# Second pass of a split-precision attention score on 64 rows: two matmuls, one for each bank, with keys' and queries' parts doubled

## Chip, cores and metric

One core of a Trainium2 chip runs the kernel. The metric is the device time of one execution in microseconds; the median of three runs of the kernel before is 688.32 us (688.25 to 689.17).

## What is computed

One pre-norm residual layer with stick-breaking attention, and a final RMSNorm. 1024 tokens, width 1024, 16 heads of 64, all in float32.

```python
def stick_breaking_attention(q, k, v):          # per head, for each block of 128 queries
    z = jnp.einsum('bhqd,bhkd->bhqk', qb, kf) * d ** -0.5
    log_beta = jax.nn.log_sigmoid(z)
    log_1m = jnp.where(mask, log_beta - z, 0.0)              # mask: key before query
    after = lax.cumsum(log_1m, axis=3, reverse=True) - log_1m
    a = jnp.where(mask, jnp.exp(log_beta + after), 0.0)
    return jnp.einsum('bhqk,bhkd->bhqd', a, vf)

def sb_mixer(h, w_in, w_out):
    q, k, v, gate = jnp.split(h @ w_in, 4, axis=-1)
    o = stick_breaking_attention(heads(q), heads(k), heads(v))
    return (o * jax.nn.silu(gate)) @ w_out

x = x + sb_mixer(rmsnorm(x, norm_g), w_in, w_out)
return rmsnorm(x, final_g)
```

## The kernel before

**Precision.** Every float32 operand of a product is held as a high part, rounded to float32r, and a low part, the difference. A product is the sum of float32r matmuls: high by high, high by low, low by high. For the projections these are three matmuls of 128 rows (`project`, L522). For the scores a head has only 64 rows (HD = 64), so high and low part lie one above the other on 128 partitions: `q_of(par, hh)` holds the high part of q of head hh on rows 64 hh to 64 hh + 63 and the low part on the other 64. `k_of(par, hh, False)` is laid out in the same way; `k_of(par, hh, True)` is the same with its halves exchanged. One matmul with each gives high by high plus low by low, and high by low plus low by high.

**Staging.** Heads go in pairs, p = 0 to 7 (par = p % 2 picks one of two buffers in `arena`). A pair has 16 slots: slot s has head hh = s // 8 and query block i = s % 8 of 128 queries, with 128 (i + 1) keys; these are the widths of the scores. Each slot interleaves the scores of that block, a third of a projection of the next pair (k, v, q, then gate; 12 matmuls of 512 columns), transposes of earlier attention weights (`t_ps`) and their products with v (`o_ps`). All engines walk the slots in the order that is written in the code, each with its own queue, and wait on counting semaphores. The helper `over_pairs` runs slot 0 to 15 for pair 0, for pairs 1 to 6 in a loop, for pair 7, and a tail. In pair 7 (545 to about 605 us in the profile) there is no next pair to project, and output projections fill the slots.

**Scores** (`scores`, L618): the block's queries are the stationary operand, keys stream. The result `z_ps[s % 2]` has two banks of 512 columns; `chunks` cut the width at the bank border. Block 4 (640 keys) starts at column 256, so that its parts have 256 and 384 columns; block 5 has 512 and 256, block 6 512 and 384, block 7 512 and 512. Per bank there are two matmuls, with `k_of(..., False)` and `k_of(..., True)`: four for each of blocks 4 to 7.

**After the scores** ScalarE takes two sigmoids of z (L847, L849), VectorE a running product (L1075), GpSimd the product of both (L1211), whose result PE transposes (L681); ScalarE (L832) and VectorE (L1044) take the transposes out of `t_ps` as high and low part for the product with v (L669).

**Splitting k and q.** ScalarE evacuates a projection to `stage` (L757) and writes the high part (L777; at the start VectorE does, L975); VectorE writes the low part, two heads in two instructions (`heads_lo`, L986). That counts `qk_split`: 4 a pair, k's two halves first, q's two last. SyncE then exchanges the halves of k by four DMAs of 256 KB (`swap_k`, L398), after `qk_split` for both halves of k and after the scores of the pair before last. It does so in slot 5 for the next pair, and once before slot 0 for pair 0.

**SyncE's queue** carries in this order: loads of x and of the first weights; `swap_k(0, 0)`; then per slot the weight load of slots with s % 4 < 2 (`load_w`, L388, which waits until GpSimd, L1178, has released the buffer), stores of outputs in slots 3 and 7 (L424), `swap_k` in slot 5. Loaded weights are split by ScalarE in slots with s % 4 in (1, 2) (L784) and GpSimd (L1178).

Of the kernel before, what the change touches and what calls it, by code (L numbers as in the profile page):

```python
# [18 lines left out]
F32 = mybir.dt.float32  # L19
F32R = mybir.dt.float32r  # L20
U8 = mybir.dt.uint8

P = 128
D = 1024
S = 1024
HEADS = 16
HD = D // HEADS
PAIRS = HEADS // 2
KB = D // P
HALF = 512  # L30
GQ = HALF // P
SLOTS = 16
# [45 lines left out]
def is_tail(p):  # L78
    return isinstance(p, int) and p == PAIRS


def is_first(p):
    return isinstance(p, int) and p == 0


def wait(eng, sem, value):

    if not isinstance(value, int) or value > 0:
        eng.wait_ge(sem, value)
# [94 lines left out]
def z_offset(i):  # L184

    return 2 * P if P * (i + 1) == HALF + P else 0


def stick_breaking_layer(nc, x, norm_g, w_in, w_out, final_g, out):
# [3 lines left out]
    with ExitStack() as ctx:  # L193
        def sb(name, shape, dt=F32):
            return ctx.enter_context(nc.sbuf_tensor(name, shape, dt))
# [4 lines left out]
        def sem(name):  # L200
            return ctx.enter_context(nc.semaphore(name))
# [6 lines left out]
        w_raw = sb("w_raw", [P, 2, HALF])  # L208
        a_g = [sb("a_group0", [P, GQ, HALF]), sb("a_group1", [P, GQ, S])]
        aT = sb("aT", [P, 2, 2, HALF], F32R)  # L210
        aT_pad = sb("aT_pad", [P, 2, 2 * P], F32R)
        stage = sb("stage", [P, 2, HALF])
        gate = sb("gate", [P, S])
# [21 lines left out]
        def q_of(par, hh):  # L235
            return arena[:, par, 0, hh * S:(hh + 1) * S]

        def k_of(par, hh, swapped):
            return arena[:, par, 2 if swapped else 1, hh * S:(hh + 1) * S]

        def v_of(par):
            return arena[:, par, 3, :].rearrange("p (b x d) -> p b x d", b=KB, x=4)
# [32 lines left out]
        qk_split = sem("qk_split")  # L275
        gate_sig = sem("gate_sig")
        gate_ready = sem("gate_ready")
        k_swapped = sem("k_swapped")
        z_ready = sem("z_ready")
        rest_ready = sem("rest_ready")  # L280
        beta_ready = sem("beta_ready")
# [100 lines left out]
        def _(sp):  # L382
            wo_v = w_out.rearrange("(b p) n -> b p n", p=P)

            def load_w(n, half, buf, columns):

                wait(sp, w_ready, n - 1)
                sp.dma_start(w_raw[:, buf, :], w_in[bass.ds(columns, 1), half, :, :]  # L388
                             .rearrange("a p n -> (a p) n")).then_inc(w_loaded[buf], 16)

            def swap_k(p, par):

                sp.wait_ge(qk_split, 4 * p + 2)

                wait(sp, z_ready, SLOTS * p - SLOTS)
                for hh in range(2):
                    for to in range(2):
                        sp.dma_start(k_of(par, hh, True)[HD * to:HD * to + HD, :].bitcast(F32),  # L398
                                     k_of(par, hh, False)[HD * (1 - to):HD * (1 - to) + HD, :].bitcast(F32)
                                     ).then_inc(k_swapped, 16)  # L400

            for b in (1, 3):
                load_x_block(sp, b)
# [6 lines left out]
                        load_x_block(sp, b)  # L410
            for half in range(2):
                load_w(2 * UNITS0 + half, half, half, KB + 1)
            swap_k(0, 0)

            def slot(p, par, s):
                if s % 4 < 2 and not (isinstance(p, int) and p >= PAIRS - 1):
                    m = s // 4
                    columns = p + (2 * KB + 1, 1, 3 * KB, KB + 2)[m]
                    load_w(2 * (UNITS0 + 1 + m) + 8 * p + s % 4, s % 4, s % 4, columns)
                if s in (3, 7) and not is_first(p) and not is_tail(p):  # L420
                    half = s // 4
                    sp.wait_ge(o_lo, 2 * p - 1 + half)
                    for dram, hl in ((o_hi_dram, 0), (o_lo_dram, 1)):
                        sp.dma_start(dram[bass.ds(p - 1, 1), :, half * HALF:(half + 1) * HALF]  # L424
                                     .rearrange("a p n -> (a p) n"),
                                     o_split[:, hl, :].bitcast(F32)).then_inc(o_stored, 16)
                if s == 5 and not (isinstance(p, int) and p >= PAIRS - 1):
                    swap_k(p + 1, 1 - par)

            for s in range(SLOTS):  # L430
                slot(0, 0, s)
# [86 lines left out]
        def _(pe):  # L518
            def project(ring, bank, half, b):

                for n, (wl, hl) in enumerate(((0, 0), (0, 1), (1, 0))):
                    mm = nc.tensor.matmul(bank[:, :], w_split[:, ring, wl, b, :],  # L522
                                          hT[:, hl, b, half * HALF:(half + 1) * HALF],
                                          start=(b == 0 and n == 0), stop=(b == KB - 1 and n == 2))
                return mm
# [28 lines left out]
            for h, (kind, half) in enumerate(PROLOGUE):  # L554
                unit = "kvq".index(kind)
                wait(pe, stage_ready, h - 1)
                for b in range(KB):
                    pe.wait_ge(xt_lo, KB * half + b + 1)
                    pe.wait_ge(w_ready, 2 * unit + b // 4 + 1)
                    mm = project(unit % 2, (proj_ps, o_ps)[h % 2], half, b)  # L560
# [10 lines left out]
            def project_out(n, b, piece=0):  # L571

                nh, tokens = n // KB, slice((n % KB) * P, (n % KB + 1) * P)
                at = ORDER.index(n) + piece
                cols = pieces_of(n)[piece]
                partial = n < PARTIAL_TILES and b < PAIRS - 1
                last = PAIRS - 2 if partial else KB - 1
                first = PAIRS - 1 if n < PARTIAL_TILES and not partial else 0
                if n == 0 and partial or n == ORDER[0] and b == KB - 1 or n == KB:
                    pe.wait_ge(wo_ready, n // KB * KB + b + 1)  # L580
                if n in (0, GQ) and b < PAIRS - 1:
                    pe.wait_ge(o_loaded[n // GQ][b], 32)
                if n == ORDER[0] and b == PAIRS - 1:
                    pe.wait_ge(o_lo, 2 * PAIRS)
                if b == first:


                    if n == 0 and partial:
                        pe.wait_ge(stage_ready, 2 * UNITS0 + 8 * (PAIRS - 1) + 2)
                    elif partial or at == 0:  # L590
                        pe.wait_ge(partial_sum, n)
                    elif at < BANKS:
                        pe.wait_ge(beta_ready, SLOTS * PAIRS)
                    else:
                        pe.wait_ge(y_sum, at - BANKS + 1)
                bank = proj_ps if partial else y_banks[at % BANKS]
                for m, (ol, wl) in enumerate(((0, 0), (0, 1), (1, 0))):
                    mm = nc.tensor.matmul(bank[:, cols], hT[:, ol, b, tokens], w_out_of(nh, wl)[:, b, cols],  # L598
                                          start=(b == first and m == 0), stop=(b == last and m == 2))
                if partial and b == last:  # L600
                    mm.then_inc(partial_done, 1)
                return mm

            def scores(p, par, s):

                hh, i = s // 8, s % 8
                width = P * (i + 1)
                if s == 0:
                    pe.wait_ge(qk_split, 4 * p + 4)
                    pe.wait_ge(k_swapped, 64 * p + 64)  # L610
                    if is_first(p):
                        pe.wait_ge(xt_lo, 2 * KB)
                wait(pe, beta_ready, SLOTS * p + s - 1)
                z, q, first = z_ps[s % 2], q_of(par, hh)[:, i * P:(i + 1) * P], z_offset(i)
                for c in range(0, first + width, HALF):
                    c0, c1 = max(c, first), min(c + HALF, first + max(width, 2 * P))
                    for swapped in (False, True):
                        mm = nc.tensor.matmul(z[:, c0:c1], q, k_of(par, hh, swapped)[:, c0 - first:c1 - first],  # L618
                                              start=not swapped, stop=swapped)
                mm.then_inc(z_ready, 1)  # L620

            def project_part(p, s):
# [14 lines left out]
            def slot(p, par, s):  # L637
# [3 lines left out]
                if not is_tail(p):  # L641

                    for block in {0: (s, s + 1), 1: ()}.get(s % 8, (s,)):
                        scores(p, par, block)
# [45 lines left out]
            for n in ORDER:  # L690
                for piece in range(len(pieces_of(n))):
                    for b in range(PAIRS - 1 if n in [*ORDER[:BANKS], *range(PARTIAL_TILES)] else 0, KB):
                        mm = project_out(n, b, piece)
# [207 lines left out]
        def _(dve):  # L901
# [76 lines left out]
            def heads_lo(kind, par, half, buf, count):  # L978

                dve.wait_ge(qk_hi, count)  # L980
                cols = slice(half * HALF, (half + 1) * HALF)
                for hh in range(2):
                    rows = slice(HD * hh, HD * hh + HD)
                    other = slice(HD - HD * hh, 2 * HD - HD * hh)
                    to = q_of(par, hh) if kind == "q" else k_of(par, hh, False)
                    last = nc.vector.tensor_tensor(to[other, cols], stage[rows, buf, :],  # L986
                                                   to[rows, cols].bitcast(F32), ALU.subtract)
                last.then_inc(qk_split, 1)

# [256 lines left out]
```

## Time and profile before

| | us |
|---|---|
| median of three runs | 688.32 |
| the profiled execution | 689.03 |
| its span (first to last instruction) | 686.9 |
| PE busy | 668.6 (97%) |
| VectorE (DVE) busy | 476.6 (69%) |
| ScalarE (ACT) busy | 427.1 (62%) |
| GpSimd (POOL) busy | 280.3 (41%) |

The profile gives each engine's busy time, the span in 40 slices with the granted TensorE clock, the chain of work that ended last, and the groups of instructions; the trace behind it answers by stretch, by line and in order of time. PE is the matmuls, PEld the weight loads, which overlap them. A matmul's record runs from its start to its modelled end and overlaps the next one, so busy time of PE is no measure of its pace; distances between starts are. In views in order of time neighbouring instructions of one line are merged, and the row carries their number.

### The profile page before, as it was taken

What the parts mean: (1) busy time and instruction counts of PE and PEld (TensorE: products, weight loads), DVE (VectorE), ACT (ScalarE), POOL (GpSimd) and SP (SyncE); (2) the same over time, 40 slices, a digit from 0 to 9 for tenths busy, and PEclk for the clock granted to TensorE, in tenths of its full rate; (3) what the DMA queues carried; (4) which work ended last, traced back from release to release, by engine and by line L of the source; (5) the groups of instructions that cost most, each with busy time, mean ns of one, the idle gap of its engine ahead of it and who ended that gap; (6) DMA issues with size and microseconds to landing.
All of it is one profiled execution on the core that took longest, in us unless ns stands there. A gap on an engine that the chain in (4) does not pass through costs nothing.

```text
span 686.9 us, 10934 instructions
## 1 busy us (share of the span) xinstructions
PE 668.6 (97%) x3450; PEld 564.6 (82%) x3450; DVE 476.6 (69%) x619; ACT 427.1 (62%) x798; POOL 280.3 (41%) x225
## 2 busy tenths in 40 slices
PE   5999999999999999999999999999999989999996
PEld 5787888888888888888888888888888877888885
DVE  4835666786777667766777676867686799755555
ACT  5714767676767676766676767666666775532533
POOL 2131434444455445453635263535362544345000
PEclk9999999999999999999999999999999999999999
DMA  7131311141004201411141013210231168531332
GB/s 292 45 92 47 93 31 31 48 133 36 23 24 131 70 18 32 122 61 31 31 123 61 31 32 109 75 31 27 83 89 46 53 198 296 173 123 43 128 142 101
DMA packets 28123, 57.65 MB, mean 84 GB/s; under 512 B 3376, under 2 KB 3504, under 8 KB 28080
## 3 DMA queue, kind: packets, MB, share of 16 engines
q1 hardware_dynamic: 25312, 51.22, 24.6%
q10 hardware_dynamic: 2736, 5.94, 2.3%
q8 instruction: 16, 0.26, 0.2%
q14 instruction: 27, 0.22, 0.1%
q0 software_dynamic: 32, 0.00, 0.0%
HBM read 37.23 MB, written 11.53 MB: 71 GB/s over the span
## 4 chain that ended last, share of the span: by engine, by line
PE 91%; DVE 4%; ACT 2%; DMA 1%; issue 1%; POOL 1%; ACTq 0%; POOLq 0%; DVEq 0%
PE proj_ps L522 46%; PE o_ps L669 10%; PE z_ps L618 9%; PE t_ps L681 9%; PE z_ps L598 8%; PE proj_ps L598 4%; PE o_ps L522 2%; DVE rest L1075 2%; PE t_ps L531 1%; PE z_ps L550 1%; DVE hT L937 1%; DMA a_group<-x 1%; POOL a_group L1211 1%; PE z_ps L542 1%; ACT rest L847 0%
## 5 line engine op out<-in xcount | busy, mean ns | idle before, releaser
L522 PE MATMUL proj_ps<-hT,w_split 128*128 128x512 f32 x1464 | 360.2, 394 | 1.8 <-DVE hT L937 1.1
L522 PEld LDWEIGHTS proj_ps<-hT,w_split 128*128 128x128 f32 x1464 | 270.0, 188 | 57.4 <-DVE hT L937 2.0
L1211 POOL TENSOR_TENSOR a_group<-a_group,rest 128x128 f32<-128x128 f32 (+7 forms) x128 | 158.2, 1236 | 300.1 <-DVE rest L1075 300.1
L1075 DVE TENSOR_TENSOR_SCAN rest<-rest,restart 128x128 f32<-128x128 f32 (+7 forms) x128 | 206.5, 1614 | 15.8 <-ACT rest L847 15.2
L832 ACT ACTIVATE aT<-t_ps 128x512 fp32r<-128x512 f32 (+2 forms) x160 | 80.1, 532 | 61.4 <-PE t_ps L681 60.0
L1044 DVE TENSOR_TENSOR aT<-t_ps,aT 128x512 fp32r<-128x512 f32 (+2 forms) x160 | 93.1, 607 | 33.1 <-ACT aT L832 31.8
L1178 POOL TENSOR_TENSOR w_split<-w_raw,w_split 128x512 fp32r<-128x512 f32 x64 | 91.2, 1426 | 37.3 <-DVE w_split L903 37.3
L618 PE MATMUL z_ps<-arena 128*128 128x512 f32 (+2 forms) x384 | 96.3, 366 | 0.3 <-DVE arena L986 0.3
L986 DVE TENSOR_TENSOR arena<-stage,arena 64x512 fp32r<-64x512 f32 x64 | 43.9, 686 | 67.7 <-ACT arena L777 67.1
L847 ACT ACTIVATE rest<-z_ps 128x128 f32<-128x128 f32 (+7 forms) x128 | 83.8, 655 | 9.3 <-PE z_ps L618 9.0
L849 ACT ACTIVATE a_group<-z_ps 128x128 f32<-128x128 f32 (+7 forms) x128 | 84.4, 659 | 0.0
L681 PE MATMUL t_ps<-ident,a_group 128*128 128x128 f32 x576 | 83.8, 272 | 0.6 <-POOL a_group L1211 0.6
L669 PE MATMUL o_ps<-aT,arena 128*128 128x512 f32 (+2 forms) x320 | 81.0, 359 | 2.4 <-DVE aT L1044 2.4
L681 PEld LDWEIGHTS t_ps<-ident,a_group 128*128 128x128 f32 x576 | 68.9, 140 | 8.6 <-issue 0.9
L757 ACT ACTIVATE stage<-proj_ps 128x512 f32<-128x512 f32 x61 | 36.5, 599 | 60.7 <-PE proj_ps L522 60.7
L669 PEld LDWEIGHTS o_ps<-aT,arena 128*128 128x128 f32 x320 | 59.6, 188 | 16.3 <-DVE aT L1044 4.1
L618 PEld LDWEIGHTS z_ps<-arena 128*128 128x128 f32 x384 | 59.6, 190 | 5.1 <-DVE arena L986 0.8
L598 PE MATMUL z_ps<-arena,hT 128*128 128x512 f32 (+1 forms) x270 | 60.9, 382 | 0.0
L598 PEld LDWEIGHTS z_ps<-arena,hT 128*128 128x128 f32 x270 | 48.7, 188 | 9.3
L824 ACT ACTIVATE oT<-o_ps 64x512 f32<-64x512 f32 x32 | 19.0, 593 | 59.9 <-PE o_ps L669 59.9
L1034 DVE TENSOR_TENSOR oT<-o_ps,oT 64x512 f32<-64x512 f32 x32 | 22.0, 688 | 25.0 <-ACT oT L824 24.6
L784 ACT ACTIVATE w_split<-w_raw 128x512 fp32r<-128x512 f32 x56 | 35.8, 640 | 0.5
(96 smaller groups left out, 450.2 us busy)
## 6 DMA issues: line engine op xcount, KB each, us to landing
w_raw<-w_in SPq DMA_DIRECT2D x64, 256.0 KB, 2.6
arena<-arena SPq DMA_DIRECT2D x32, 256.0 KB, 4.3
wo_raw<-w_out SPq DMA_DIRECT2D x16, 256.0 KB, 4.1
o_hi_scratch<-o_split SPq DMA_DIRECT2D x14, 256.0 KB, 2.1
o_lo_scratch<-o_split SPq DMA_DIRECT2D x14, 256.0 KB, 2.5
hT<-o_hi_scratch SPq DMA_DIRECT2D x14, 256.0 KB, 5.3
hT<-o_lo_scratch SPq DMA_DIRECT2D x14, 256.0 KB, 6.2
a_group<-x SPq DMA_DIRECT2D x13, 256.0 KB, 3.1
```

The lines of the kernel that those rows point to most:

```text
L522: mm = nc.tensor.matmul(bank[:, :], w_split[:, ring, wl, b, :], hT[:, hl, b, half * HALF:(half + 1) * HALF], start=(b == 0 and n == 0), st ...
L598: mm = nc.tensor.matmul(bank[:, cols], hT[:, ol, b, tokens], w_out_of(nh, wl)[:, b, cols], start=(b == first and m == 0), stop=(b == last ...
L618: mm = nc.tensor.matmul(z[:, c0:c1], q, k_of(par, hh, swapped)[:, c0 - first:c1 - first], start=not swapped, stop=swapped)
L669: mm = nc.tensor.matmul(o_ps[:, c:HALF], v_of(apar)[:, j, 2 * ahh:2 * ahh + 2, :] .rearrange("p x d -> p (x d)"), moving, start=(j == 0 an ...
L681: last = nc.tensor.transpose(t_ps[t % 2][:, i2 * P:(i2 + 1) * P], a_g[grp][:, i2, j * P:(j + 1) * P], ident[:, :])
L832: nc.scalar.activation(to, t_ps[t % 2][:, rel * P:HALF], ACT.Copy).then_inc(t_hi, 1)
L847: nc.scalar.activation(rest[:, s % 2, S - width:S], z_ps[s % 2][:, first:first + width], ACT.Sigmoid, scale=-SCALE).then_inc(rest_ready, 1)
L849: nc.scalar.activation(a_g[grp][:, i % GQ, 0:width], z_ps[s % 2][:, first:first + width], ACT.Sigmoid, scale=SCALE).then_inc(beta_ready, 1)
L1044: nc.vector.tensor_tensor(lo, t_ps[t % 2][:, rel * P:HALF], hi.bitcast(F32), ALU.subtract).then_inc(t_lo, 1)
L1075: nc.vector.tensor_tensor_scan(span, span, restart[:, S - 1:(S - 1 - width if width < S else None):-1], 0.0, ALU.mult, ALU.max).then_inc(s ...
L1178: nc.gpsimd.tensor_tensor(to[:, 1], w_raw[:, part, :].rearrange("p (b n) -> p b n", b=4), to[:, 0].bitcast(F32), ALU.subtract).then_inc(w_ ...
L1211: nc.gpsimd.tensor_tensor(a, a, rest[:, s % 2, S + 1 - width:S + 1], ALU.mult).then_inc(a_ready, 1)
```

## The change

The two layouts of k become "high part twice" (`k_of(..., False)`) and "low part twice" (`k_of(..., True)`), each on 128 rows. VectorE writes the low part of k into the second layout instead of under the high part; four DMAs copy each half to the other rows (`double_k` in place of `swap_k`, same places in the queue, same sizes). A first pass against the high parts gives (high q + low q) by high k. For blocks 0 to 3 the second pass against the low parts is again a matmul on 128 rows. For blocks 4 to 7 it takes only high q by low k on 64 rows: one matmul for each bank, the first on rows 0 to 63, the second on rows 64 to 127. For that the high part of q is needed on both row halves: a new tile `q_twins` gets the missing half for queries 512 to 1023 by two DMAs of 128 KB a pair (`double_q`), queued on SyncE after `double_k(0, 0)` for pair 0 and at slot 15 for each next pair; PE waits for it at block 4. The order of matmuls in all blocks of two banks changes from bank by bank to pass by pass. The scratch for software DMAs is set to 4096 bytes, which makes room for `q_twins`.

```diff
+        q_twins = sb("q_twins", [P, 2, HALF], F32R)
...
+        def q_twin(par, hh):
+
+            return q_twins[HD - HD * hh:2 * HD - HD * hh, par, :]
...
-            def swap_k(p, par):
+            def double_k(p, par):
 
                 sp.wait_ge(qk_split, 4 * p + 2)
 
                 wait(sp, z_ready, SLOTS * p - SLOTS)
                 for hh in range(2):
-                    for to in range(2):
-                        sp.dma_start(k_of(par, hh, True)[HD * to:HD * to + HD, :].bitcast(F32),
-                                     k_of(par, hh, False)[HD * (1 - to):HD * (1 - to) + HD, :].bitcast(F32)
-                                     ).then_inc(k_swapped, 16)
+                    for lower in range(2):
+                        have = (hh + lower) % 2
+                        k = k_of(par, hh, bool(lower))
+                        sp.dma_start(k[HD * (1 - have):HD * (1 - have) + HD, :].bitcast(F32),
+                                     k[HD * have:HD * have + HD, :].bitcast(F32)).then_inc(k_doubled, 16)
+
+            def double_q(p, par):
+
+                sp.wait_ge(qk_split, 4 * p + 4)
+                wait(sp, z_ready, SLOTS * p - SLOTS)
+                for hh in range(2):
+                    sp.dma_start(q_twin(par, hh).bitcast(F32),
+                                 q_of(par, hh)[HD * hh:HD * hh + HD, HALF:S].bitcast(F32)).then_inc(q_doubled, 16)
...
-            swap_k(0, 0)
+            double_k(0, 0)
+            double_q(0, 0)
...
-                    swap_k(p + 1, 1 - par)
+                    double_k(p + 1, 1 - par)
+                if s == 15 and not (isinstance(p, int) and p >= PAIRS - 1):
+                    double_q(p + 1, 1 - par)
...
-                for c in range(0, first + width, HALF):
-                    c0, c1 = max(c, first), min(c + HALF, first + max(width, 2 * P))
-                    for swapped in (False, True):
-                        mm = nc.tensor.matmul(z[:, c0:c1], q, k_of(par, hh, swapped)[:, c0 - first:c1 - first],
-                                              start=not swapped, stop=swapped)
+                chunks = [(max(c, first), min(c + HALF, first + max(width, 2 * P)))
+                          for c in range(0, first + width, HALF)]
+                for lower in (False, True):
+                    if lower and i >= GQ:
+                        break
+                    for c0, c1 in chunks:
+                        mm = nc.tensor.matmul(z[:, c0:c1], q, k_of(par, hh, lower)[:, c0 - first:c1 - first],
+                                              start=not lower, stop=lower)
+                if i >= GQ:
+
+                    if i == GQ:
+                        pe.wait_ge(q_doubled, 32 * p + 32)
+                    for half, (c0, c1) in enumerate(chunks):
+                        rows = slice(HD * half, HD * half + HD)
+                        upper = q[rows, :] if half == hh else q_twin(par, hh)[:, (i - GQ) * P:(i - GQ + 1) * P]
+                        mm = nc.tensor.matmul(z[:, c0:c1], upper, k_of(par, hh, True)[rows, c0 - first:c1 - first],
+                                              start=False, stop=True)
...
-                    last = nc.vector.tensor_tensor(to[other, cols], stage[rows, buf, :],
+                    lower = q_of(par, hh) if kind == "q" else k_of(par, hh, True)
+                    last = nc.vector.tensor_tensor(lower[other, cols], stage[rows, buf, :],
                                                    to[rows, cols].bitcast(F32), ALU.subtract)
...
-    nc = _bacc.Bacc("TRN2", target_bir_lowering=False, num_devices=1)
+    nc = _bacc.Bacc("TRN2", target_bir_lowering=False, num_devices=1, dynamic_dma_scratch_size=4096)
```

## Rows read from the trace of the kernel before

**Rows 1.** The page: busy shares, granted clock in 40 slices, chain by engine.

```profile
PE 668.6 (97%) x3450; PEld 564.6 (82%) x3450; DVE 476.6 (69%) x619; ACT 427.1 (62%) x798; POOL 280.3 (41%) x225
...
PEclk9999999999999999999999999999999999999999
...
PE 91%; DVE 4%; ACT 2%; DMA 1%; issue 1%; POOL 1%; ACTq 0%; POOLq 0%; DVEq 0%
```

**Rows 2.** Stretches: length, busy of PE, PEld, DVE, ACT, POOL, clock, DMA.

```profile
306.00:324.00 18.00, 18.00 (x97) 15.43 (x96) 11.53 (x16) 12.85 (x24) 6.36 (x6) 1.00 0.11 30
...
558.00:576.00 18.00, 15.53 (x80) 12.40 (x79) 17.43 (x16) 13.98 (x26) 7.91 (x5) 1.00 0.87 299
```

**Rows 3.** PE's waits, 62 to 545 us, then 545 to 612: total, times, longest.

```profile
PE proj_ps L522 <- ACT stage L757: 0.7, 2, 0.4
...
PE o_ps L669 <- DVE aT L1044: 2.4, 2, 1.8
```

**Rows 4.** Groups by form, 89 to 545 us: busy, mean ns of one, idle.

```profile
L522 PE MATMUL proj_ps<-hT,w_split 128*128 128x512 f32 x1244 | 304.8, 394 | 0.0
...
L522 PEld LDWEIGHTS proj_ps<-hT,w_split 128*128 128x128 f32 x1242 | 229.6, 188 | 46.2
```

**Rows 5.** PE in order of time at block 7: start, us, engine and line.

```profile
329.07 0.51 PE L669 MATMUL o_ps<-aT,arena 128*128 128x384 f32 x2
329.42 0.38 PE L681 MATMUL t_ps<-ident,a_group 128*128 128x128 f32 x2
329.56 1.17 PE L618 MATMUL z_ps<-arena 128*128 128x512 f32 x4
330.56 2.88 PE L522 MATMUL proj_ps<-hT,w_split 128*128 128x512 f32 x12
333.28 0.40 PE L669 MATMUL o_ps<-aT,arena 128*128 128x256 f32 x2
333.51 0.27 PE L681 MATMUL t_ps<-ident,a_group 128*128 128x128 f32 x1
```

**Rows 6.** The same view: eight transposes before block 3, and block 4.

```profile
307.02 1.03 PE L681 MATMUL t_ps<-ident,a_group 128*128 128x128 f32 x8
307.81 0.59 PE L618 MATMUL z_ps<-arena 128*128 128x384 f32 x2
...
316.92 0.83 PE L618 MATMUL z_ps<-arena 128*128 128x256 f32 x4
317.59 2.91 PE L522 MATMUL proj_ps<-hT,w_split 128*128 128x512 f32 x12
```

**Rows 7.** All engines in order of time at the start of pair 0.

```profile
45.73 3.30 SPq L398 DMA_DIRECT2D arena<-arena  x4
...
49.08 2.74 SPq L388 DMA_DIRECT2D w_raw<-w_in  x2
...
58.04 1.39 DVE L986 TENSOR_TENSOR arena<-stage,arena 64x512 fp32r<-64x512 f32 x2
...
62.22 0.65 ACT L784 ACTIVATE w_split<-w_raw 128x512 fp32r<-128x512 f32 x1
...
63.73 2.55 PE L522 MATMUL proj_ps<-hT,w_split 128*128 128x512 f32 x10 [0.40 <-ACT stage L757]
```

**Rows 8.** DMA issues: count, KB each, median us from issue to landing.

```profile
w_raw<-w_in SPq DMA_DIRECT2D x64, 256.0 KB, 2.6
arena<-arena SPq DMA_DIRECT2D x32, 256.0 KB, 4.3
```

**Rows 9.** In order of time, pair 1 to 2: q's last split, the weight load for slot 0, block 4.

```profile
176.91 1.39 DVE L986 TENSOR_TENSOR arena<-stage,arena 64x512 fp32r<-64x512 f32 x2 [2.46 <-ACT arena L777]
...
187.23 0.33 SPq L388 DMA_DIRECT2D w_raw<-w_in  x1
...
210.76 0.83 PE L618 MATMUL z_ps<-arena 128*128 128x256 f32 x4
```

**Rows 10.** A stretch of 4.5 us in a pair, columns as in rows 2.

```profile
284.00:288.50 4.50, 4.50 (x26) 3.88 (x26) 4.28 (x6) 3.19 (x6) 2.52 (x2) 1.00 0.88 224
```

More of the change, by code:

```diff
@@ L277, in stick_breaking_layer @@
         gate_ready = sem("gate_ready")
-        k_swapped = sem("k_swapped")
+        k_doubled = sem("k_doubled")
+        q_doubled = sem("q_doubled")
         z_ready = sem("z_ready")
@@ L609, in scores @@
                     pe.wait_ge(qk_split, 4 * p + 4)
-                    pe.wait_ge(k_swapped, 64 * p + 64)
+                    pe.wait_ge(k_doubled, 64 * p + 64)
                     if is_first(p):
```

## The prediction

> **What bounds the kernel now.** I read the page first: busy shares, then the chain that ended last, then the TensorE clock [rows 1]. TensorE (PE) is busy 668.6 of 686.9 us, 91% of the chain is PE, and the granted clock digit is 9 in all 40 slices, so a saving is priced at one clock. VectorE and ScalarE have 69% and 62%. A mean hides stages, so next come stretches of 18 us [rows 2]: from 306 to 324 us, inside a pair, PE has no idle time, while VectorE is busy 11.53 of 18; in the last pair of heads (558 to 576) PE falls to 15.53, and there VectorE has 17.43. Then PE's waits [rows 3]: from 62 to 545 us it stood still 0.7 us in all; in 545 to 612 its longest entry is 2.4 us for VectorE. So from the first score to 545 us, time taken out of PE's stream comes out of the total, and in the last pair only part of it.
>
> **What a matmul costs here.** A record's duration is no price, since matmuls overlap: a 512-column matmul has 394 ns [rows 4], but twelve of them lie between the starts 330.56 and 333.28 us [rows 5], 0.227 us each. In the same rows two of 384 columns take 329.42 - 329.07 = 0.35 (0.175 each) and two of 256 take 333.51 - 333.28 = 0.23 (0.115 each). So PE pays for columns, and the weight load (188 ns on its own record [rows 4]) is hidden under the matmul before. Where matmuls are short, loads set the pace: eight transposes of 128 columns from 307.02 to 307.81 [rows 6], plus the 0.08 us by which the next record starts early, give 0.109 each. That 0.08 is seen at the score blocks: 512-column block 7 lasts 1.00 from its start to the next one [rows 5], and 4 x 0.227 is 0.91. Block 4 lasts 317.59 - 316.92 = 0.67, by columns 2 x 0.115 + 2 x 0.175 = 0.58 [rows 6]. The prices hold.
>
> **The change on PE.** Per head only query blocks 4 to 7 change: two full matmuls stay (one per bank), and two full ones of the second pass become two on 64 rows each, in different row halves and banks. If these run side by side, the pair costs its longer one. One thing can delay it: two weight loads must go in under the last full matmul, and a load takes 0.109. Block 5 (512 and 256): 2 x (0.227 + 0.115) = 0.684 becomes 0.342 + 0.227, gain 0.115. Block 6 (512 and 384): gain 0.175. Block 7: gain 0.227. Block 4 (256 and 384): the last full matmul starts at 0.115, the two loads end at 0.333, the 384 columns behind them end at 0.508, against 0.580: gain 0.072. Together 0.589 us per head. Pairs 0 to 6 are 14 heads: 8.25 us. In the last pair I count nothing for its first head, whose slots stand on VectorE [rows 2, 3], and 0.59 for the second: 8.8 us in all. Adding the first head back is the upper end, 9.4.
>
> **The price of changing over.** The unknown is what it costs to go from a 128-row matmul to 64-row ones and back, twice per block. No row shows a 64-row matmul. Below nothing is excluded, because the columns are counted already. The nearest row is another change of form, from fp32 transposes to the scores' matmuls, 128 rows both: blocks 4 and 7 cost no more than their columns and the 0.08 that belongs to the transposes before [rows 5, 6], so that change costs 0. The far end is that the array waits until the matmul in flight is out: 0.394 - 0.227 = 0.167 each [rows 4, 5]. I take 0, as nearest, and keep 0.167 for the range. On PE-bound ground there are 60 blocks (14 heads and one of the last pair), so 120 changeovers: 20.0 us at the far end. The sum turns over at (8.8 - 2.0) / 120 = 0.057 us each, the 2.0 being the next two terms.
>
> That change of transposes to matmuls shows no drain. The Trainium skill (TensorEngine Tiling (Array Packing), Key Properties) says that changing the tiling mode, and not just the tile, drains the TensorE; it gives no price. No run here shows it yet. By that rule the far end is the likelier, which is the first rival below.
>
> **Start of the layer.** SyncE's queue gets the doubling of q behind that of k, ahead of the weight load for slot 0. Doubling q waits for the last split of q, on VectorE from 58.04 to 59.43; today the four copies of k are issued from 45.73 in 3.30 us and the weight loads at 49.08 [rows 7]. After: two copies from 59.43 at 3.30 / 4 = 0.83 each, the weight load at 61.1, landed 2.6 us later [rows 8] at 63.7. ScalarE splits that tile at 62.22 and only then evacuates the projection, for which PE already waits until 63.73 [rows 7]. So ScalarE and PE slip 1.5 us. Bounds: 0, if the load lands sooner, and 3.2, if it comes behind the q copies' 4.3 us [rows 8]. I take 1.5.
>
> **Steady pairs.** Doubling q is placed after slot 15. The last split of q is done at 176.91 + 1.39 = 178.3, and the weight load behind it in the queue, that of the next pair's slot 0, goes at 187.23 and not sooner, since it waits for GpSimd to release its buffer [rows 9]. Two issues of 0.83 fit; the twin is needed at 210.76 [rows 9]. If that cover were gone, each pair would lose up to 1.7 us. The copies of k keep their number, size and place; VectorE's low parts of k go to another address at the same cost; PE's new wait for the twin is met long before and has no work held behind it. The smaller scratch for DMAs touches one small load at the start. All these are 0.
>
> **Stalls of a faster PE.** In 284 to 288.5, among the fullest stretches of a pair, VectorE is busy 4.28 of 4.5 us [rows 10]; block 5 lies in it and takes 0.115 from PE, which leaves 4.385, so VectorE still does not bind, but a short wait can appear. I take 0.5 us for all pairs (0 to 2).
>
> Sum: -8.8 + 1.5 + 0.5 = -6.8 us. The profiled execution took 689.03 (span 686.9 and 2.1 around it) and would be 682.2; the median 688.32 lies 0.7 below it, so I forecast 681.5.
>
> **Rivals.** *First, changeovers drain:* each waits 0.167, and the total is 688.3 - 8.8 + 20.0 + 1.5 = 701.0. It decides from 0.057 each upward; at half the price it gives 691. For it: the array would have to let sums over 128 rows pass out before it is divided, and no row shows a changeover that divides it. Against it: no cost at transposes. A worse form: weight loads cannot go ahead of the changeover either, another 0.109 each, 714. *Second, not side by side:* the two 64-row matmuls run one after the other; they then cost the full columns, nothing is gained and the start costs its 1.5: 689.8. The change does not do what it says. For it: no row shows two matmuls sharing the array. *Third, VectorE takes over* when PE speeds up: at most the 2 us above, 683.
>
> Side by side itself rests on a page alone: the Trainium skill (TensorE: Matmul & The Clock Gate, Measured speedup vs the span model) has four 32-row matmuls of 512 columns 3.07 times faster together; no row here shows it.
>
> **How the numbers follow.** Forecast, with the third rival in it: 0.50 (own range 679 to 687.5: from 9.4 gained and no stall to 0.05 per changeover). Drain: 0.27 (691 to 702); its worse form: 0.07. One after the other: 0.10 (689 to 690.5). Around no change, a changeover near 0.057: 0.06. The range 679 to 702 leaves out the worst form and a little at either end. About 0.2% (1.4 us) is what a measurement of this kernel can tell from no change. Faster by more: 0.50; within: 0.08 (0.06 and a small part of the second rival); slower: 0.42.
>
> **What would show it.** Right: in blocks 4 to 7 the two 64-row matmuls start at most about 0.11 us apart, a block 7 lasts some 0.77 from its start to the next instead of 1.00, and PE's wait that ends at 63.73 today grows from 0.4 to some 1.9 us. Drain: a gap beyond 0.227 between the last full matmul and the first 64-row one, and again before the projection. One after the other: 0.227 between the starts of the pair. Wrong at the start: no later evacuation near 63 us.

## The result, and the profile after

The changed kernel takes 702.08 us (701.77 to 702.51), before beside it 688.31: a ratio of 1.0195, 95% interval 1.0183 to 1.0207, 13.8 us slower. The time forecast was 681.5, and 702.08 lies just outside the range that reached 702.0. The first rival, that changing over between 128 and 64 rows drains the array, had 701.0.

The page after, beside [rows 1]: busy shares, granted clock, chain by engine and by line.

```profile
span 700.4 us, 10966 instructions
PE 682.3 (97%) x3450; PEld 553.3 (79%) x3450; DVE 474.3 (68%) x619; ACT 428.2 (61%) x798; POOL 280.2 (40%) x225
...
PEclk9999999999999999999999999999999999999999
...
PE 92%; DVE 4%; ACT 1%; DMA 1%; issue 1%; SPq 0%; ACTq 0%; DVEq 0%
```

The same number of matmuls and weight loads, the same clock, and still a chain of PE: the span grew by 13.5 us, PE's busy time by 13.7, and the weight loads' busy time fell. So the loss lies in PE's own stream, while it counts as busy. The view in order of time shows where. This is block 7, the counterpart of [rows 5], matmuls first and then the weight loads (PEld) of the same stretch; the last column is idle time before.

```profile
337.60 0.71 PE L639 MATMUL z_ps<-arena 128*128 128x512 f32 x2
338.24 0.50 PE L648 MATMUL z_ps<-arena,q_twins 64*128 64x512 f32 x1
338.24 0.50 PE L648 MATMUL z_ps<-arena 64*128 64x512 f32 x1
338.67 2.56 PE L540 MATMUL proj_ps<-hT,w_split 128*128 128x512 f32 x10
...
337.57 0.30 PEld L639 LDWEIGHTS z_ps<-arena 128*128 128x128 f32 x2
338.23 0.18 PEld L648 LDWEIGHTS z_ps<-arena,q_twins 64*128 64x128 f32 x1 [0.36 <-issue]
338.24 0.18 PEld L648 LDWEIGHTS z_ps<-arena 64*128 64x128 f32 x1
338.67 2.36 PEld L540 LDWEIGHTS proj_ps<-hT,w_split 128*128 128x128 f32 x11 [0.25 <-issue]
```

What to see: the two 64-row matmuls start together, so they do share the array. But the block lasts 338.67 - 337.60 = 1.07 us to its next matmul, against 1.00 before. Two full matmuls take 338.24 - 337.60 - 0.08 (what the transposes before leave over) = 0.56, where 2 x 0.227 = 0.45 would do: 0.10 too much. The pair then takes 338.67 - 338.24 = 0.43, where one matmul has 0.227: 0.20 too much. The excess goes on behind the block: the twelve projection matmuls take 341.52 - 338.67 = 2.85 us from their first start to the next line's, where the kernel before has 333.28 - 330.56 = 2.72 [rows 5]: 0.13 too much. Together 0.43, and with the 0.227 saved a net loss of 0.20 us at block 7.

The PEld rows tell why. These are the weight loads of the kernel before at its block 7:

```profile
329.53 0.76 PEld L618 LDWEIGHTS z_ps<-arena 128*128 128x128 f32 x4
330.34 0.64 PEld L522 LDWEIGHTS proj_ps<-hT,w_split 128*128 128x128 f32 x3
```

There a weight load starts right after the matmul ahead of it has started: the projection's first load at 330.34, 0.22 before its matmul. Here the loads of the pair start only at 338.23, together with their matmuls' records, and so does the first load of the projection at 338.67. The line's own view counts it for all blocks:

```profile
L648 PEld LDWEIGHTS z_ps<-arena,q_twins x64: 182/183/183, 71.6 to 616.5; 64*128 64x128 f32 x64
...
  issue: 17.8, 64
```

64 visits to the 64-row form, and 17.8 us of idle weight-load engine before them that no semaphore explains, 0.28 each.

Second, the start of the layer, beside [rows 7]:

```profile
59.87 1.10 SPq L414 DMA_DIRECT2D q_twins<-arena  x2
...
61.02 1.08 SPq L394 DMA_DIRECT2D w_raw<-w_in  x2
...
64.04 0.63 ACT L814 ACTIVATE w_split<-w_raw 128x512 fp32r<-128x512 f32 x1 [1.27 <-DMA w_raw<-w_in]
64.58 0.58 ACT L787 ACTIVATE stage<-proj_ps 128x512 f32<-128x512 f32 x1
...
65.21 3.03 PE L540 MATMUL proj_ps<-hT,w_split 128*128 128x512 f32 x12 [1.46 <-ACT stage L787]
```

The weight load goes at 61.02 instead of 49.08, ScalarE waits 1.27 us for it, and PE's wait grows from 0.40 to 1.46.

Third, the last pair. Block 4 of its first head and block 0 of its second, in order of time, first before and then after:

```profile
558.53 0.83 PE L618 MATMUL z_ps<-arena 128*128 128x256 f32 x4
...
572.92 0.72 PE L618 MATMUL z_ps<-arena 128*128 128x256 f32 x4
```

```profile
571.52 0.54 PE L639 MATMUL z_ps<-arena 128*128 128x256 f32 x2
...
585.91 0.71 PE L639 MATMUL z_ps<-arena 128*128 128x256 f32 x4
```

Both lie 13.0 us later than before, so the four visits between them add nothing. A view by stretch tells why, with the columns of [rows 2]:

```profile
571.00:589.00 18.00, 16.30 (x80) 11.64 (x79) 17.43 (x16) 13.97 (x26) 7.91 (x5) 1.00 0.88 299
```

VectorE is busy 17.43 of 18 us, to the digit as in the counterpart in [rows 2]; PE waits for it there anyway, and its new delay goes into that wait.

### The profile page after: what moved, and what is told of

It reads as the page before. It is cut to its first block, busy times and chain, and to the rows that moved or that the text cites. A ratio compares the mean times of both kernels' runs of the same rounds, so it can differ in the third digit from the quotient of the medians.

```text
span 700.4 us, 10966 instructions
## 1 busy us (share of the span) xinstructions
PE 682.3 (97%) x3450; PEld 553.3 (79%) x3450; DVE 474.3 (68%) x619; ACT 428.2 (61%) x798; POOL 280.2 (40%) x225
## 4 chain that ended last, share of the span: by engine, by line
PE 92%; DVE 4%; ACT 1%; DMA 1%; issue 1%; SPq 0%; ACTq 0%; DVEq 0%
PE proj_ps L540 47%; PE o_ps L699 10%; PE t_ps L711 9%; PE z_ps L616 8%; PE z_ps L639 6%; PE proj_ps L616 4%; PE z_ps L648 3%; PE o_ps L540 2%; PE t_ps L549 1%; PE z_ps L568 1%; DVE rest L1106 1%; DVE hT L967 1%; DMA a_group<-x 1%; PE z_ps L560 1%; DMA w_raw<-w_in 0%
## 5 line engine op out<-in xcount | busy, mean ns | idle before, releaser
L540 PE MATMUL proj_ps<-hT,w_split 128*128 128x512 f32 x1464 | 365.7, 398 | 2.8 <-ACT stage L787 1.6
L540 PEld LDWEIGHTS proj_ps<-hT,w_split 128*128 128x128 f32 x1464 | 267.2, 188 | 68.8 <-issue 12.5
L639 PE MATMUL z_ps<-arena 128*128 128x512 f32 (+2 forms) x256 | 72.0, 372 | 0.3 <-DVE arena L1017 0.3
L639 PEld LDWEIGHTS z_ps<-arena 128*128 128x128 f32 x256 | 37.8, 190 | 1.0 <-DVE arena L1017 0.8
```

The lines of the kernel that those rows point to most:

```text
L639: mm = nc.tensor.matmul(z[:, c0:c1], q, k_of(par, hh, lower)[:, c0 - first:c1 - first], start=not lower, stop=lower)
```

## Experiments

Theory: each changeover between 128-row and 64-row matmuls costs a fixed time, once for the array to run empty and once for a weight load that cannot be hidden. Rivals: the doubling with its DMAs, or the order of the passes, costs it; or the sharing of the array does, two streams slowing each other. Diffs are against the changed kernel.

**All rows, with and without doubling of q.**

```diff
                 for lower in (False, True):
-                    if lower and i >= GQ:
-                        break
                     for c0, c1 in chunks:
...
-                    for half, (c0, c1) in enumerate(chunks):
-                        rows = slice(HD * half, HD * half + HD)
-                        ...
```

and for the second also

```diff
-            double_q(0, 0)
...
-                if s == 15 and not (isinstance(p, int) and p >= PAIRS - 1):
-                    double_q(p + 1, 1 - par)
```

> The layouts, the doubling of k and of q, and the order pass by pass as in the changed kernel, but the second pass of blocks 4 to 7 runs as two matmuls on all 128 rows. It computes one product more (low q by low k), nothing is left out. Theory of the changeover: all of the loss but that at the start is gone, 688.3 + 1.1 (the stall at the start that the trace of the changed kernel shows) = 689.4 us. Rival, that doubling, its DMAs or the order of passes cost it: it stays near 700.

> As e1_all_rows, and q is not doubled at all. Theory: the stall at the start comes from the weight load behind the doubling of q in SyncE's queue, so this is the time of before, 688.3 (688.0 to 688.7). If the stall comes from the doubling of k instead: 689.4.

Measured: 690.32 us (ratio 1.0031, interval 1.0019 to 1.0042) and 689.24 us (1.0012, 1.0003 to 1.0022), before beside both 688.46. So 12 of the 13.8 us leave with the 64-row matmuls: neither the DMAs nor the order of passes cost more than a small rest. The doubling of q costs the 1.1 us between the two. Against the kernel before beside them both are some 0.8 us higher than expected, and the interval of the second leaves out no change. Most of it can be found: block 5 with the projection behind it takes 3.56 to 3.57 us from start to start in both runs, 3.53 to 3.54 before, in both heads of every pair read (100 to 545 us). A steady pair takes 0.07 us more, seven pairs 0.5. As the second run has no doubling of q, this belongs to the order pass by pass or to the layout of k; the rest, 0.3, stays open.

**The doubling of q behind the first weight loads.**

```diff
             double_k(0, 0)
-            double_q(0, 0)
...
             for s in range(SLOTS):
                 slot(0, 0, s)
+                if s == 1:
+                    double_q(0, 0)
```

> The changed kernel, with the doubling of q for pair 0 behind the weight loads of slots 0 and 1 in SyncE's queue. Theory: 702.1 - 1.1 = 701.0, and PE's wait near 65 us falls from 1.5 to 0.4 us. If those loads are not the cause: 702.1.

Measured: 700.96 us, 1.1 less. PE's waits from 55 to 545 us:

```profile
PE proj_ps L541 <- ACT stage L788: 0.6, 2, 0.4
```

The longest fell from 1.5 to 0.4. The stall at the start is the place in SyncE's queue and nothing else.

**One behind the other, on the same 64 rows.**

```diff
-                        rows = slice(HD * half, HD * half + HD)
-                        upper = q[rows, :] if half == hh else q_twin(par, hh)[:, (i - GQ) * P:(i - GQ + 1) * P]
+                        rows = slice(HD * hh, HD * hh + HD)
+                        upper = q[rows, :]
```

> The changed kernel, but both 64-row matmuls of a block use the same 64 rows (those where the high part of q lies anyway), so they cannot share the array. Theory of the changeover (two per block stay, the sharing goes): per head 0.115 + 0.115 + 0.175 + 0.227 = 0.63 us more, 15 heads, 702.1 + 9.5 = 711.6. Rival, that the loss comes from the sharing itself, the two streams slowing each other: the pair took 0.43 us side by side, so one behind the other costs about the same, 702 to 703. If there were no sharing in the changed kernel either: 702.1.

Measured: 712.11 us. The sharing gave its 9.5 us, to within 0.6. Block 7 in order of time:

```profile
342.17 0.71 PE L639 MATMUL z_ps<-arena 128*128 128x512 f32 x2
342.81 0.72 PE L648 MATMUL z_ps<-arena 64*128 64x512 f32 x2
343.46 1.89 PE L540 MATMUL proj_ps<-hT,w_split 128*128 128x512 f32 x7
```

Until the 64-row matmuls 342.81 - 342.17 = 0.64, as in the changed kernel. The two together take 0.65, that is 0.43 + 0.22: the second one adds its columns alone, and its load is hidden again.

**Bank by bank: four changeovers, the same matmuls.**

```diff
-                for lower in (False, True):
-                    ...
+                rows = slice(HD * hh, HD * hh + HD)
+                for c0, c1 in chunks:
+                    for lower in (False, True):
+                        r = rows if lower and i >= GQ else slice(0, P)
+                        mm = nc.tensor.matmul(z[:, c0:c1], q[r, :], k_of(par, hh, lower)[r, c0 - first:c1 - first],
+                                              start=not lower, stop=lower)
```

> The matmuls of e4_one_behind_other in the order full, 64-row, full, 64-row: four changeovers a block in place of two, everything else equal. Theory: the trace of the changed kernel gives 0.39 to 0.41 us for two changeovers, 60 blocks on PE's path, so 23.4 to 24.6 us above e4_one_behind_other: 711.6 + 24 = 735.6. If changing over were free: 711.6, as e4.

Measured: 736.29 us, 24.2 above the run before it, with the same four matmuls a block. Over 60 blocks on PE's path that is 0.40 us for two changeovers, 0.20 each; over all 64 it would be 0.38 and 0.19. Block 7 now takes 355.61 - 353.91 = 1.70 us:

```profile
353.91 1.76 PE L641 MATMUL z_ps<-arena 128*128 128x512 f32 x4
355.61 3.01 PE L540 MATMUL proj_ps<-hT,w_split 128*128 128x512 f32 x12
```

This is the run that decides: the matmuls are the same, and only their order, with it the number of changeovers, moved. That a bank is written twice in a row is not the cause: the kernel before has that order too, on 128 rows, and its block 7 costs no more than its columns [rows 5].

**Only block 7, only block 4.** The condition `i >= GQ` of the second pass becomes `i == 7`, and `i == 4`; the others run on all rows.

> Only block 7 of each head has its second pass on 64 rows, side by side; blocks 4 to 6 run on 128 rows. Theory: 689.4 + 15 heads x 0.20 = 692.4. Rival, a loss in proportion to the columns on 64 rows: block 7 would have the largest share of the 12.4 us, some 4.

> Only block 4 has its second pass on 64 rows. Theory: the price of two changeovers is the same as at block 7, but only 0.115 us of columns are saved against 0.227, so 689.4 + 15 x 0.27 = 693.5, more than with block 7 alone. Rival, in proportion to columns: less than with block 7 alone, some 692.

Measured: 691.21 us (ratio 1.0040, 1.0026 to 1.0054) and 693.46 us (1.0079, 1.0062 to 1.0095). The totals have the order that the theory wants, but not its sizes. Both expectations stood on 689.4 for the kernel with all rows, which measured 690.3. Over that, block 7 alone adds 0.9 us where 3.0 was expected, and block 4 alone 3.1 where 4.1 was; that block 4 meets its 693.5 is two errors that cancel. Distances between starts settle it. With block 4 alone, block 4 and the projection behind it take 3.69 us, with all rows 3.43: a net loss of 0.26, and with 0.115 of columns saved a price of 0.38. With block 7 alone, block 7 and its projection take 3.91 in the first head and 3.93 in the second, with all rows 3.76 and 3.73: 0.15 and 0.20 lost, with 0.227 saved a price of 0.38 and 0.43. So the price hardly depends on the columns, and the visit that streams fewer of them loses more.

That block 7 looks so cheap in the total has another reason, which the weight loads' waits from 89 to 560 us show. First with block 4 alone, then the same in the kernel before; with block 7 alone there is no such row left:

```profile
PEld o_ps L698 <- DVE aT_pad L1074: 1.6, 5, 0.3
```

```profile
PEld o_ps L669 <- DVE aT_pad L1044: 1.8, 6, 0.3
```

Once a pair, after the second head's block 7, PE came 0.2 to 0.3 us too early for VectorE. A delay just ahead of that place is absorbed, about 0.17 us of it a pair; with block 4 alone, whose delay comes four slots earlier, the wait stays as it was. The steady pairs below add 0.18 and 0.53 us for the two visits of a pair, so seven pairs would give 1.3 and 3.7 where the totals have 0.9 and 3.1; with block 4 alone, 0.4 us of the profiled execution's share lies ahead of the first score, which starts at 58.63 and with all rows at 59.01; the rest of the difference stays open.

**The pair twice.** The product of high q and low k is added twice here.

```diff
-                    for half, (c0, c1) in enumerate(chunks):
+                    for turn, (half, (c0, c1)) in enumerate(2 * list(enumerate(chunks))):
...
-                                              start=False, stop=True)
+                                              start=False, stop=turn >= 2)
```

> The changed kernel with the pair of 64-row matmuls run twice in a row in blocks 4 to 7, so that high q by low k is added twice. Theory: inside a visit a further pair costs its longer matmul alone, 0.175 + 3 x 0.227 = 0.856 a head, 15 heads, 702.1 + 12.8 = 714.9. If a pair always costs the 0.37 to 0.43 us that it takes in the changed kernel: 702.1 + 15 x 1.65 = 726.9. If its weight loads stay in the open even inside a visit: 714.9 + 60 x 0.109 = 721.4.

Measured: 714.45 us, 12.4 above the changed kernel. Block 7:

```profile
343.38 0.50 PE L648 MATMUL z_ps<-arena,q_twins 64*128 64x512 f32 x1
343.38 0.50 PE L648 MATMUL z_ps<-arena 64*128 64x512 f32 x1
343.71 0.39 PE L648 MATMUL z_ps<-arena,q_twins 64*128 64x512 f32 x1
343.72 0.39 PE L648 MATMUL z_ps<-arena 64*128 64x512 f32 x1
344.04 3.01 PE L540 MATMUL proj_ps<-hT,w_split 128*128 128x512 f32 x12
```

This splits the price. The first pair takes 0.33 = 0.11 (its load in the open) + 0.227, and its records have 0.50 us; the second has the 0.39 of any hidden load. From the second pair to the projection 0.33 = 0.227 + 0.10. That the array runs empty in these 0.10 us is a reading: what the rows show is that no column and no load is taken in. Inside the 64-row form everything has the pace that the plan counted on.

**All runs by the steady pair.** The distance from block 4 of the first head in pair 3 to the same in pair 4 leaves out the start and the last pair, and the steady pairs of one run agree in it to 0.04 us. It was read from the trace of each run:

| kernel | starts | distance, us |
|---|---|---|
| before | 281.30, 351.85 | 70.55 |
| all rows | 282.14, 352.76 | 70.62 |
| block 7 alone | 282.48, 353.28 | 70.80 |
| block 4 alone | 283.15, 354.30 | 71.15 |
| changed kernel | 287.73, 359.93 | 72.20 |
| one behind the other | 291.18, 364.74 | 73.56 |
| the pair twice | 291.40, 365.30 | 73.90 |
| bank by bank | 300.15, 376.85 | 76.70 |

A pair has eight blocks with 64-row matmuls. From one behind the other to bank by bank it grows by 3.14 us for 16 more changeovers, 0.20 each. The sharing is worth 1.36, or 0.68 a head, and the second 64-row pair costs 1.70, or 0.85 a head, where 0.63 and 0.856 were expected.

## Why the prediction was wrong, point by point

**The bound** was right: PE's stream set the time, and what was added to it came out of it, in the last pair's first head not at all.

**What a matmul costs** was right, and so was the sharing: two 64-row matmuls start together, in every block, and running them one behind the other costs 10.0 us against 9.5 by the distances between starts. One detail was off: I let the pair's two loads follow each other (block 4 at 0.072 saved); they go in together (their starts lie 0.01 apart), so the saving is 0.115 and 0.63 a head.

**The price of changing over is the step that failed.** I took 0 us a changeover from the nearest row, the change between transposes and scores' matmuls. That row changes what runs on 128 rows and never divides them, so it was near in form and said nothing on the question. The runs give 0.20 us each: 0.10 before the next weight load starts, in which the array would run empty, and 0.11 for that load in the open. My far end of 0.167 was too high for the first part and left the second out, which stood only in the "worse form"; that form, with both at their full size, had 714. That the first rival's 701.0 lies so near to 702.08 is therefore in part luck: its price of 0.167 comes near 0.20 only because one part too large stands for two. The point from which a changeover costs more than it saves was put at 0.057; the measured price is over three times that.

The account with measured sizes: two changeovers are 0.39 us a block on the mean (0.37 to 0.43 by block), less 0.115, 0.115, 0.175 and 0.227 saved, 0.91 a head and 1.82 a pair. About 0.17 of that goes into the wait for `aT_pad`, which leaves the 1.65 us that a steady pair has grown. Seven pairs are 11.6; on it come 0.5 for the last pair's second head and 1.1 for the start: 13.2. The span has 13.5, and 0.4 of it lies ahead of the first score (59.48 before, 59.90 after), where the profiled executions differ by more than that: the same score starts at 58.63 with block 4 alone, at 59.01 with all rows and at 59.63 with the doubling of q moved.

The rule that was weighed against the trace holds. The Trainium skill (TensorEngine Tiling (Array Packing), Key Properties) says that a change of tiling mode drains the TensorE; the runs agree and put 0.10 us to it. On the load, the row of after comes first: the columns of the two full matmuls are through at 337.60 + 0.08 + 0.45 = 338.13, and the next load starts at 338.23. The Trainium skill (TensorE: Matmul & The Clock Gate, The mechanism, "What overlaps and what doesn't") lets a weight load overlap a matmul only where the row groups differ. This trace has it otherwise: loads on the same 128 rows are hidden throughout the kernel before, and they come into the open exactly at a changeover. That fits another sentence of the same section of the Trainium skill, by which a load into the background weight buffer may also go ahead of matmuls in flight.

**The start** was right in mechanism and place, and slightly too dear: 1.5 foreseen, 1.1 measured, twice (with and without the doubling of q, and with it moved). The landing was right by two errors that cancel. Taking off the 0.4 us by which this execution is late from before the first score, the load was issued 0.5 sooner than foreseen (SyncE issued the two copies in 1.10 us and not 1.66), but 3.0 us passed to ScalarE's start and not 2.6. What the sum left out is slack on ScalarE, which before stood still for 0.21 us between its split and its evacuation:

```profile
63.09 0.60 ACT L757 ACTIVATE stage<-proj_ps 128x512 f32<-128x512 f32 x1 [0.21 <-PE proj_ps L522]
```

From the split's start to the evacuation's it was 63.09 - 62.22 = 0.87 before and 64.58 - 64.04 = 0.54 after, and so 0.3 of the slip did not reach PE.

**Steady pairs** were right: no wait for the twin or for weights on PE after the start. **Stalls of a faster PE** were not tested, since PE became slower; the opposite showed, a wait that takes up lateness.

**The second and third rivals** are out: the matmuls do run side by side, and VectorE did not take over. **The chances** put 0.50 on the forecast and 0.34 on the two forms of a drain. Where the only row for a cost is of another kind and a stated rule names the cost, the rule deserved the larger part.

No version here beats the kernel before. A visit would have to save over 0.4 us; the widest block saves 0.227, and all four of a head in one visit 0.63, for which their scores would have to stand in PSUM at once, eight banks where `z_ps` has four. That was not tried.

## What to carry to other kernels

Splitting the array's rows pays by the visit, not by the matmul: count the changeovers, here 0.20 us each, and gather enough 64-row work between two of them that half its columns are worth more than 0.4 us. When an operation has no row in the trace, ask of the nearest row whether it contains the very thing that is new; if it doesn't, it is no reason to take its value. A transfer that waits for late data goes behind those in its queue that are needed sooner.

## What the runs showed of the hardware that I had not expected

Two 64-row matmuls on different row halves start within 0.01 us of each other, and so do their weight loads. At a changeover nothing of the next weight load is hidden: its 0.11 us come on top of 0.10 us in which neither columns nor a load go in, in both directions (0.11 and 0.13 in the open at block 7). PE counts as busy through all of it, 97% before and after; only the distance between starts and the idle time of PEld ("issue", 17.8 us before 64 loads) show the loss.
